# Odd layer's head rows: squares, scale and turn started three token blocks behind their products, with PSUM banks of their own

## The reference

```
q, k, v = split(h @ w_in)          # 512 latent tokens, 1024 -> 3 x 1024
qc, kc, vc = split(hc @ w_in)      # 256 context tokens
q = _rms(q, q_g); k = _rms(k, k_g) # per head: x * rsqrt(mean(x*x) + 1e-6) * g
o = _neighbourhood_attention(q, k, v, kc, vc, rel_bias) @ w_out
```

## Time and profile before

| | |
|---|---|
| three runs | 3852.33, 3855.22, 3859.16 us, median 3855.22 |
| the profiled execution | 3854.43 us, its span in the trace 3852.5 us |
| busy share of the span | PE 94%, PE weight loads 76%, DVE 53%, ACT 37%, POOL 4% |
| mean granted PE clock | 0.966 |
| odd layer's projections | about 3070 to 3292 us of the span |

### The profile page before, as it was taken

The page is one execution under the profiler, slowest core; times in us unless marked ns, Lnnn a source line. Parts: engine busy times, 40 slices in busy tenths (PEclk is TensorE's granted clock), DMA queues, the critical chain, the costliest instruction groups (busy, mean ns, idle before and its releaser), DMA issues.

```text
span 3852.5 us, 49219 instructions
## 1 busy us (share of the span) xinstructions
PE 3631.7 (94%) x19410; PEld 2909.0 (76%) x19410; DVE 2052.7 (53%) x3673; ACT 1431.0 (37%) x2223; POOL 160.7 (4%) x270
## 2 busy tenths in 40 slices
PE   8899999999998999999999889899999989899999
PEld 6676677787776766778777766788888789677887
DVE  4645666777756456577885554432232442654333
ACT  3445642443134456424431344321212233643222
POOL 0000000000000000000000110100000131000000
PEclk9989999999999899999999899899999999999999
DMA  4111234334421112333343100011111111211222
GB/s 170 62 55 66 75 116 144 115 120 153 175 102 60 72 50 82 116 137 127 138 158 137 73 34 1 34 60 53 68 67 54 62 67 56 69 53 69 106 93 82
DMA packets 65943, 339.95 MB, mean 88 GB/s; under 512 B 6832, under 2 KB 8368, under 8 KB 39984
## 3 DMA queue, kind: packets, MB, share of 16 engines
q1 hardware_dynamic: 65712, 336.82, 24.3%
HBM read 328.40 MB, written 8.39 MB: 87 GB/s over the span
## 4 chain that ended last, share of the span: by engine, by line
PE 72%; DVE 18%; ACT 7%; issue 2%; DMA 1%; POOL 0%; DVEq 0%; ACTq 0%; SPq 0%; POOLq 0%
PE ps L1776 21%; PE ps L1777 20%; PE ps L1778 20%; DVE wl L2027 4%; PE ps L1765 3%; DVE junk L2072 3%; PE ps L1899 2%; PE ps L1785 2%; ACT wh L1918 2%; DVE ha L2035 1%; DVE tt L2035 1%; DVE hl L2035 1%; DVE u L2027 1%; DVE mg L2027 1%; DVE pb L2253 1%
## 5 line engine op out<-in xcount | busy, mean ns | idle before, releaser
L2027 DVE TENSOR_TENSOR wl<-raw,wh 128x2048 fp32r<-128x2048 f32 (+2 forms) x275 | 545.5, 1983 | 408.6 <-ACT wh L1918 389.6
L1918 ACT ACTIVATE wh<-raw 128x2048 fp32r<-128x2048 f32 (+2 forms) x275 | 457.1, 1662 | 803.0 <-PE ps L1778 799.4
L1776 PE MATMUL ps<-hh,wh 128*128 128x512 f32 (+1 forms) x1184 | 428.3, 362 | 12.2 <-DVE hl L2035 7.9
L1778 PE MATMUL ps<-hh,wl 128*128 128x512 f32 (+1 forms) x1184 | 422.7, 357 | 0.0
L1777 PE MATMUL ps<-hl,wh 128*128 128x512 f32 (+1 forms) x1184 | 422.2, 357 | 0.0
L1776 PE MATMUL ps<-xhb,wh 128*128 128x512 f32 x832 | 369.1, 444 | 11.0 <-DVE xlb L2027 10.9
L1777 PE MATMUL ps<-xlb,wh 128*128 128x512 f32 x832 | 337.1, 405 | 0.0
L1778 PE MATMUL ps<-xhb,wl 128*128 128x512 f32 x832 | 336.1, 404 | 0.0
L1776 PE MATMUL ps<-xha,wh 128*128 128x512 f32 x704 | 280.2, 398 | 3.9 <-DVE wl L2027 3.8
L1777 PE MATMUL ps<-xla,wh 128*128 128x512 f32 x704 | 278.6, 396 | 0.0
L1778 PE MATMUL ps<-xha,wl 128*128 128x512 f32 x704 | 278.5, 396 | 0.0
(11 more groups left out here) (295 smaller groups left out, 7029.1 us busy)
## 6 DMA issues: line engine op xcount, KB each, us to landing
raw<-in_wts SPq DMA_DIRECT2D x199, 1024.0 KB, 4.8
lt<-in_wts SPq DMA_DIRECT2D x110, 512.0 KB, 3.4
raw<-in_wts SPq DMA_DIRECT2D x44, 512.0 KB, 3.4
raw<-in_wts SPq DMA_DIRECT2D x28, 448.0 KB, 3.2
x_scratch<-xt SPq DMA_DIRECT2D x3, 2048.0 KB, 10.9
xt<-x_scratch SPq DMA_DIRECT2D x3, 2048.0 KB, 8.1
oe<-in_relb SPq DMA_DIRECT2D x16, 384.0 KB, 3.4
bt<-in_big SPq DMA_DIRECT2D x1, 2688.0 KB, 8.9
```

Of the source, the lines that this page charges most:

```text
L1776: T.matmul(u.out, u.sh, u.mh, start=u.first, stop=False)
L1778: i = T.matmul(u.out, u.sl, u.mh, start=False, stop=u.last)
L1918: A.activation(u.h, u.raw, ACT.Copy).then_inc(*act.inc())
L2027: V.tensor_tensor(o_, a, b, op).then_inc(*dve.inc())
```

## The change

`FR` is replaced, for these rows alone, by two rings: products take banks 0 to 4 (`ROWS`), turned rows take bank 5 (`TURNED`). `Heads` gets a lag: a tile is kept back in `waiting` and pushed when more than `lag` tiles are waiting. The lag is 0 in the even layer and 3 in the odd one, so there the product of tile n is followed by squares(n-3), scale(n-4) and turn(n-5). At the value panels each tile first pushes one waiting tile; when none waits, the row is ended.

```
+            ROWS, TURNED = Ring(banks[0:5]), Ring(banks[5:6])
...
-                def __init__(self):
-                    self.n = 0
-                    self.row = []
+                def __init__(self, lag):
+                    self.n, self.lag = 0, lag
+                    self.row, self.waiting = [], []
                     self.u_free, self.q_free = [[], [], []], [[], []]
+
+                def add(self, *tile):
+
+                    self.waiting.append(tile)
+                    self.go_on(self.lag)
+
+                def go_on(self, most=0):
+                    while len(self.waiting) > most:
+                        self.push(*self.waiting.pop(0))
...
                 def end(self):
+                    self.go_on()
                     self.scale(self.row[-1])
...
                 def turn(self, x):
-                    u, b2 = U[x.n % 3], FR.next()
+                    u, b2 = U[x.n % 3], TURNED.next()
...
             def tm_bank(p, i, h_ks, width=256):
-                b = FR.next()
+                b = ROWS.next()
...
             def tm_first(p, h_ks, width=256):
-                bs = [FR.next() for _ in range(4)]
+                bs = [ROWS.next() for _ in range(4)]
...
-                hd, last_t = Heads(), {}                  (even)
+                hd, last_t = Heads(0), {}
...
-                hd, last_t = Heads(), {}                  (odd)
+                hd, last_t = Heads(3), {}
...
                         if q >= 8:
-                            if hd.row:
+                            if hd.waiting:
+                                hd.go_on(len(hd.waiting) - 1)
+                            elif hd.row:
                                 hd.end()
...
-                        hd.push(b, t, i, 4, None, False, place_, q < 4)
+                        hd.add(b, t, i, 4, None, False, place_, q < 4)
```

More of the change, by code:

```diff
@@ L1554, in even @@
                             b.free = [f_t]
-                hd, last_t = Heads(), {}
+                hd, last_t = Heads(0), {}
                 for q in range(3):
@@ L1572, in place_ @@
                             return last_t["q"]
-                        hd.push(b, t, i, 4 if q < 2 else 2, Q("evq") if q < 2 else Q("evk"), i < 4, place_, q < 2)
+                        hd.add(b, t, i, 4 if q < 2 else 2, Q("evq") if q < 2 else Q("evk"), i < 4, place_, q < 2)
                 def B(name):
```

## The result

The changed kernel takes 3878.69 us (median of four runs, 3877.85 to 3880.39), against 3853.77 for the kernel before in the runs beside it: a ratio of 1.0066 with a 95% interval of 1.0054 to 1.0078, or +24.9 us. The forecast was 3884.1, +29.7; the measured time lies inside the forecast range of 3868 to 3892.

A forecast was written before the change was run, and what follows sets the result against it. The prediction took PE as the bound, hurt by queue order. Panel ends +27.4, end of panel 7 +3.0 and start -0.75 gave +29.7 on 3854.43 us, 3884.1 us, range 3868 to 3892.

The forecast's parts named there:

- The direction and its cause: Odd layer's panel ends: the next product waits for a bank freed by a scale queued behind `wh`; slower overall, chance 0.90.
- The length of the wait: Product after each odd-layer panel end starts 3.6 us late, at 3119.26 instead of 3115.68, uncovered.
- The clock: PE's clock drops after each 3.6 us wait, costing 2.1 us per product; wait and clock together had chance 0.62.
- the second wait: After a panel end, scale(n-3) behind `wl` delays PE about 0.45 us at full clock, hidden behind a slow product.
- The second case: Rival: full speed after each of the seven waits, +18.2 us, 3872.6 us; chance 0.18.
- The nearer row: Profile row where the clock averaged 0.65 after a 3.86 us wait, costing 1.7 us; used throughout it gives 3881 us.
- Panel ends 1 to 6: Odd layer: 3.6 wait plus 2.1 clock less the old 1.13, 4.57 us each, six times, +27.4.
- End of the key tiles: End of panel 7: 3.6 + 2.1 + 0.7 for two turns sharing one bank, less the old 3.37, +3.0 us.
- The start: Odd layer's start: product 5 waits 8.9 us plus 2.1 of clock, 11.0 against 11.75 before, -0.75 us.
- The even layer and the steady tiles: No gain or loss in the even layer or the odd layer's steady tiles, 0 us each.
- the rival of waits in steady tiles: 0.3 us more on each of 27 tiles not at a panel's start, +8 on top, 3892 us; chance 0.10.
- the faster rival: All panel-end waits go if scale(n-4) ends in time, -10.9 us, 3843.5 us; chance 0.05.

The follow-up runs named there:

- e2: Changed kernel with the odd layer's lag set to 2 instead of 3, five product banks kept: 3846.6 us, ratio 0.9980 to the kernel before.
- e3: Changed kernel with a sixth bank in the odd layer's ring for products, lag 3 kept: 3849.3 us, ratio 0.9983 to the kernel before.
- e1: Changed kernel with the odd layer's lag set back to 0, the two rings kept: 3851.9 us, ratio 0.9994 to the kernel before.
- e6: Changed kernel with six product banks and the odd layer's scale emitted ahead of the squares, lag 3: 3840.9 us, ratio 0.9966 to the kernel before.
- e7: Changed kernel with the odd layer's lag back at 0, five banks, scale ahead of the squares: 3851.9 us, ratio 0.9997 to the kernel before.
- e5: Changed kernel, lag 3 and five banks, with the odd layer's scale emitted ahead of the squares: 3875.9 us, ratio 1.0057 to the kernel before.
- e8: Changed kernel with six banks, scale ahead of the squares and `wl` emitted one tile later in the odd layer: 3837.8 us, ratio 0.9954 to the kernel before.
- e4: Changed kernel with 24 unread identity transposes at the end of each of panels 1 to 7, where PE waits: 3868.7 us, ratio 1.0038 to the kernel before.

## Why the prediction was right, point by point

**The direction and its cause** held: the bank of product n+1 is released by the scale emitted right before it, and that scale stands behind a sum that waits for `wh`. The trace shows the chain, e2 and e3 remove the wait by slack on either side, and e1 excludes the split of the banks.

**The length of the wait**: 3.6 us forecast; first matmul at +3.70 instead of +0.14, so 3.56, at all seven ends.

**The clock**: the term that was too large. I took 2.1 us behind each of seven waits, from one product behind a wait of 8.2 us. They cost 10.3 us, 1.5 on average, because the clock stayed up behind one and came back earlier behind most. That is 4.4 us. With another 0.8 at the start, less 0.4 for the second wait that shows behind 3200, it makes the 4.8 by which the forecast change was too high. The forecast time is 5.4 too high, since the kernel before took 3853.8 beside this run and not 3854.4. The nearer row, 1.7 behind 3.86 us, would have been closer. The second case, full clock throughout, was wrong six times in seven.

**Panel ends 1 to 6**: +27.4 forecast. From turn to turn over each end, less 3.06, the lost time is 6.3, 5.1, 5.1, 5.1, 4.0 and 5.0 (a turn or two of aftermath included), 30.6 in all; less 6.8 before, +23.8.

**End of the key tiles**: +3.0 forecast, 5.1 + 0.8 - 3.4 = +2.5 measured. The 0.7 for two turns on one bank stands in the trace as the wait of 0.66 for ACT.

**The start**: -0.75 forecast. PE waits 8.84 us (8.9 forecast) before product 5, and the slow product costs 1.3 instead of 2.1; -1.5. That the wait came out so near is partly luck: scale 0 waited 0.38 us there for a POOL root of 2.93, which the forecast did not have. The three sum to 24.8, the stretch says 24.9.

**The even layer and the steady tiles**: 0 forecast. PE waits for `u` 13 times from 2180 to 2290 us, 9.6 us in all, in both kernels; between panel ends no product of the odd layer waits, and turns follow at 3.06 us, so the rival of waits in steady tiles is out. (It counted 27 products off a panel's start; panels 1 to 7 have 29, which would have made its addition 9 us.)

**What it missed**: the faster rival was priced as if an early scale would end all waits. e6 and e7 show that it would not; a held-up POOL keeps most of the second wait. The Trainium skill's reading ("Perfetto Trace Analysis", Optimization Strategy) of repeated gaps as too little SBUF or PSUM, which I gave little, is right for the changed kernel, where a sixth bank gains 29 us. It doesn't fit the kernel before, whose gaps are for `u`; no run gave that kernel another bank.

## What to carry to other kernels

When work is made to lag behind its producer, count the ring. Here a bank is released lag + 1 tiles behind the newest product, so lag + 2 banks let the kernel run and make release and next use fall into the same step (five at lag 3); lag + 3 give one tile of slack (six at lag 3, five at lag 2). Then ask not whether the inputs of the releasing instruction are old, but what stands ahead of it in its engine's queue. A lag that is one less, or a ring that is one larger, turned 25 us of loss into 5 to 8 us of gain. The further gain, from 5.7 to 11.9 us in the stretch, came with a better order on DVE and with `wl` kept off the root that PE waited for.

## What the runs showed of the hardware

**POOL is held up by `wl` on DVE.** A `tensor_tensor` of POOL on 128 x 4 takes 1.01 us. When it starts while `wl` runs (128 x 2048, 2.29 us, both operands in SBUF) it takes 2.92 to 2.93 and ends about 0.9 us after `wl`. In each of e5 to e8 this happens to eight of the forty roots, which take 55.6 us together against 40.3 before, and e8 moves the effect with `wl` from one tile to the next. The Trainium skill ("SBUF — State Buffer", two separate sides) says that a GpSimd operation and a VectorE operation with two SBUF inputs take a shared port pair exclusively, whichever starts first, and that the other blocks for the whole instruction. Where `wl` starts first this trace agrees: the root ends 0.87 us behind it. That it is the port, and not something else about `wl`, no run here separates.

In the changed kernel one root is held up too, that of tile 0:

```profile
3099.87 2.93 POOL L2289 TENSOR_TENSOR st<-st 128x4 f32<-128x4 f32 x1
```

In the kernel before none is. There the root of the panel's last tile starts 0.32 us ahead of `wl` (3119.34 in the earlier trace rows):

```profile
3119.02 1.01 POOL L2276 TENSOR_TENSOR st<-st 128x4 f32<-128x4 f32 x1
```

`wl` takes its usual 2.29 us all the same, so with POOL first the trace shows no block of either engine.

**The clock after waits of equal length.** Seven idle times of 3.33 us, each after 10 us or more of almost unbroken work, were followed by 2.7, 1.6, 1.6, 1.6, 0, 1.4 and 1.5 us of cost. With 0.7 us idle instead (e4) it never fell. The price of such a wait varies within one execution, so here only an average over several could have been forecast.
